# The second block of an expert's tokens: gathered feature-major from split rows, scaled on ScalarE and VectorE, its slots turned later

## The chip, the core and the metric

The kernel runs on one core of a Trainium2 chip. It is timed in device microseconds, as the median of several runs. Besides, one execution was taken by the hardware profiler; its page and trace tell for each engine what it did and what it waited for. The engines are PE (TensorE, with its weight loads as PEld), DVE (VectorE), ACT (ScalarE), POOL (GpSimd) and SP (SyncE, which here issues the weight transfers).

## What is computed

Three transformer layers run over 256 tokens of width 1024: one layer of a first model (grouped attention, spatial gating, cross attention), then two layers of a second model (stick-breaking attention, retention). Each of the three ends in a mixture of 16 experts, of which a token uses two. Cut to what matters here, for the second model:

```python
h = x * (1.0 + scale) + shift                    # per feature
combine = ...                                    # 256 x 16, two nonzero weights a token
for e in range(16):
    hidden = silu(t @ w_gate[e]) * (t @ w_up[e]) # 1024 -> 512
    out = out + combine[:, e:e+1] * (hidden @ w_down[e])   # 512 -> 1024
```

Per expert that is 6 MB of float32 weights, 16 x 3 panels of 2 MB in each expert stage.

## The kernel before

**Stages.** Each of the three expert stages is `moe(L)` with L = 0, 1, 2. It routes the tokens, then walks over eight pairs of experts: `pair(q, k)` with q = 0 to 3 and k = 0, 1. The pairs of q = 0 and q = 3 are written out, those of q = 1 and 2 are a loop. The order of the work is that of the code on each engine, tied together by semaphores; nothing is planned at run time but the routing.

**Slots.** An expert takes its tokens in blocks of at most 64 (`CAP`). The first block of every expert is gathered together with three others: `SELQ` holds for four experts the 0/1 selection of tokens to slots, and `gather_quad` multiplies it with the token rows. For that the normalised rows are held twice in float32r, as a high and a low part (`XHR`, `XLR`), with the features of a chunk side by side. The result comes out with features on partitions, is scaled and shifted from PSUM by ACT and DVE (`quad_out`, L1511 and L2166), and is the stationary operand of the gate and up products (`gate_up`, L871).

**The second block.** An expert with more than 64 tokens gets further blocks. After each pair every engine runs `more` for both experts of the pair (PE L994, ACT L1575, DVE L2244). It reads the number of further blocks from `TBL`, jumps over the block's code if there is none, and else loops over the blocks. DVE has made the block's selection `SELX` beforehand for every expert, needed or not (`choose_more`, L2147). A block goes like this:

1. PE: `gather_more` (L848) multiplies `SELX` with the unsplit float32 rows, which gives 64 slots on partitions by 1024 features, folded into one PSUM bank `B_XG` (4 products, which the trace shows as 8 passes).
2. PE: `turn_more_slots` (L863) turns the selection and collects the slots' weights in bank `B_TR`, for the scatter at the end.
3. ACT: copies the gathered rows to `XROWS` (L1583); later it copies the turned slots out (`swt_more_out`, L1523).
4. PE: `turn_more` (L856) transposes `XROWS` back to features on partitions, four transposes.
5. DVE: `xe_out` (L2179) scales and shifts eight chunks of 128 x 64 into `XEX` (L2186).
6. PE: `gate_up` on `XEX`, into bank `B_GU`: 16 products, in the trace 32 passes of 512 columns.
7. ACT silu (L1588), DVE multiplication (L2251), PE `turn_more_h`, ACT copy (L1590), PE `down_more`, DVE weighting (L2257), ACT and DVE split (L1594, L2263), PE `scatter_more`.

**Weights.** Six ring slots of 2 MB, `ring_lo` and `ring_hi` with three each, hold gate, up and down panels of the two experts of a pair. SP issues a panel's load (L1211) once the old panel in its slot has been read: gate and up after the block's gate and up products, where there is a block, down after its down product. SP waits in a fixed order: gate and up of the first expert, gate and up of the second, then both down panels.

**Records.** Nearly all products have line L419, the helper that issues them; they are told apart by their operands. `Z` in the names stands for one large scratch tensor that holds `SELX`, `XEX` and the hidden rows among others.

Of the kernel before, what the change touches and what calls it, by code (L numbers as in the profile page):

```python
# [20 lines left out]
F32 = mybir.dt.float32  # L21
# [7 lines left out]
P = 128  # L29
# [71 lines left out]
def build(nc, A, out, stop, final_ready):  # L101
# [40 lines left out]
    ZR, ZT = 8960, 11264  # L142
    with nc.sbuf_tensor("Z", [P, 12288], F32) as Z:
        pass
    with nc.sbuf_tensor("Z_before_SELQ", [P, 2560], F32):
        with nc.sbuf_tensor("SELQ", [P, NT, 4 * CAP], F32R) as SELQ:
            with nc.sbuf_tensor("TURN", [P, NT, TURN_COLS], F32R) as TURNER:
                pass
# [183 lines left out]
    def zv(at, *shape):  # L332
        v = Z[:, at:at + int(np.prod(shape))]
        if len(shape) == 2:
            return v.rearrange("p (a b) -> p a b", b=shape[1])
        return v
# [27 lines left out]

    RT = Z[:, 11264:12288]

    SELX = [zv(2048 + 256 * k, NT, P) for k in range(2)]
    free = [3072 + NT * TURN_COLS]

    def cols(n):  # L370
# [27 lines left out]
    def m(L, name):  # L398
        return S(f"m{L}_{name}")
# [17 lines left out]
    def _(pe):  # L417
        def mm(o, l, r, start, stop):
            return nc.tensor.matmul(o, l, r, start=start, stop=stop, skip_group_check=True)  # L419
# [339 lines left out]
        def moe(L):  # L759
# [87 lines left out]

            def gather_more(k):  # L848

                by4 = src[:, :, :].rearrange("p t (i h j) -> p t h i j", h=2, j=4)  # L850
                for t in range(NT):
                    mm(ps[0:CAP, B_XG, :], SELX[k][:, t, 0:CAP], by4[:, t, 0], t == 0, t == NT - 1)
                    ins = mm(ps[CAP:P, B_XG, :], SELX[k][:, t, CAP:P], by4[:, t, 1], t == 0, t == NT - 1)
                ins.then_inc(m(L, "x_xr"), 1)

            def turn_more():  # L856

                by4 = XROWS[:, :].rearrange("p (i j) -> p j i", j=4)
                for j in range(4):
                    ins = nc.tensor.transpose(ps[:, B_XG, j * P:(j + 1) * P], by4[:, j, :], ident)  # L860
                ins.then_inc(m(L, "x_xg"), 1)

            def turn_more_slots(k, done):  # L863
                sel = SELX[k]
                for t in range(NT):
                    ins = nc.tensor.transpose(ps[:, B_TR, t * P:(t + 1) * P], sel[:, t, :], ident)
                for t in range(NT):
                    ins = mm(ps[:, B_TR, SEQ:SEQ + 1], sel[:, t, :], WTOKX[k][:, t:t + 1], t == 0, t == NT - 1)
                ins.then_inc(done, 1)
# [124 lines left out]
            def more(p, k, a, wg, wu, wd, final):  # L994

                e = 2 * p + a
                nb = pe.value_load(TBL[0:1, L, 0, bass.ds(e, 1)], min_val=0, max_val=3)
                b1 = pe.value_load(TBL[0:1, L, 1, bass.ds(e, 1)], min_val=1, max_val=48)
                with pe.If(nb > 0):
                    with pe.Fori(0, nb) as j:  # L1000
                        if k == 0:
                            wait_moe(pe, L, "swt", p + 2)
                            wait_moe(pe, L, "ws", p + 2)
                        elif not final:
                            wait_moe(pe, L, "xe_a", p + 2)
                            wait_moe(pe, L, "xe_v", p + 2)
                        pe.wait_ge(m(L, "x_sel"), b1 + 2 * p + 1 + j)
                        gather_more(a)
                        turn_more_slots(a, m(L, "x_swp"))
                        pe.wait_ge(m(L, "x_xs"), b1 + j)  # L1010
                        turn_more()
                        pe.wait_ge(m(L, "x_xe"), b1 + j)
                        wait_moe(pe, L, "ye", 2 * p + 2)
                        gate_up(B_GU, lambda c: XEX[:, c, :], wg, wu, m(L, "x_gu"), False)
                        pe.wait_ge(m(L, "x_h"), b1 + j)
                        turn_more_h()
                        pe.wait_ge(m(L, "x_ht"), b1 + j)
                        down_more(wd, m(L, "x_y"))
                        pe.wait_ge(m(L, "x_swt"), b1 + j)
                        pe.wait_ge(m(L, "x_ye"), b1 + j)  # L1020
                        scatter_more().then_inc(m(L, "xdone"), 1)
# [265 lines left out]
    def _(act):  # L1287
# [196 lines left out]
        def moe(L):  # L1484
# [90 lines left out]
            def more(p, a):  # L1575

                e = 2 * p + a
                nb = act.value_load(TBL[0:1, L, 0, bass.ds(e, 1)], min_val=0, max_val=3)
                b1 = act.value_load(TBL[0:1, L, 1, bass.ds(e, 1)], min_val=1, max_val=48)
                with act.If(nb > 0):  # L1580
                    with act.Fori(0, nb) as j:
                        act.wait_ge(m(L, "x_xr"), b1 + j)
                        nc.scalar.activation(XROWS[:, :], ps[:, B_XG, :], Copy).then_inc(m(L, "x_xs"), 1)  # L1583
                        act.wait_ge(m(L, "x_swp"), b1 + j)
                        act.wait_ge(m(L, "xdone"), b1 + j)
                        swt_more_out(m(L, "x_swt"))
                        act.wait_ge(m(L, "x_gu"), b1 + j + 1)
                        nc.scalar.activation(SGX[CAP:P, :], ps[0:CAP, B_GU, :], ACT.Silu).then_inc(m(L, "x_sg"), 1)  # L1588
                        act.wait_ge(m(L, "x_htp"), b1 + j)
                        nc.scalar.activation(HTX.rearrange("p c s -> p (c s)"), ps[:, B_GU, 0:SEQ], Copy).then_inc(m(L, "x_ht"), 1)  # L1590
                        act.wait_ge(m(L, "x_yf" if L else "x_y"), b1 + j)
                        act.wait_ge(m(L, "x_swt"), b1 + j)
                        if L:
                            nc.scalar.activation(YH[2], SGX, Copy).then_inc(m(L, "x_yh"), 1)  # L1594
                        else:
                            nc.scalar.activation(YH[2], ps[:, B_Y, :], Copy, scale=WSLOT[2]).then_inc(m(L, "x_yh"), 1)
# [130 lines left out]
    def _(dve):  # L1727
# [336 lines left out]
        def moe(L):  # L2064
# [112 lines left out]
                ins.then_inc(S("moe_ws"), 1)  # L2177

            def xe_out(done):  # L2179
                xg = ps[:, B_XG, :].rearrange("p (j h s) -> p j h s", j=4, h=2)  # L2180
                for c in range(KC):
                    o = xg[:, c % 4, c // 4, :]
                    if shift is None:
                        ins = V.tensor_scalar(XEX[:, c, :], o, gain[:, c:c + 1], None, ALU.mult)
                    else:
                        ins = V.tensor_scalar(XEX[:, c, :], o, gain[:, c:c + 1], shift[:, c:c + 1], ALU.mult, ALU.add)  # L2186
                ins.then_inc(done, 1)
# [56 lines left out]
            def more(e, a, nb, b1):  # L2244

                with dve.If(nb > 0):
                    with dve.Fori(0, nb) as j:
                        dve.wait_ge(m(L, "x_xg"), b1 + j)
                        xe_out(m(L, "x_xe"))
                        dve.wait_ge(m(L, "x_sg"), b1 + j)  # L2250
                        V.tensor_tensor(HH[CAP:P, :], ps[CAP:P, B_GU, :], SGX[CAP:P, :], ALU.mult).then_inc(m(L, "x_h"), 1)  # L2251
                        if L:
# [340 lines left out]
```

## Time and profile before

| | us |
|---|---|
| median of 3 runs | 1489.62 |
| lowest and highest run | 1488.06, 1492.7 |
| span of the profiled execution | 1480.9 |
| PE busy in it | 1320.8 |
| DVE busy | 581.3 |
| ACT busy | 431.7 |

The page gives the profiled execution by its span, from the first to the last instruction; what lies around it is the rest of the device time. A row of the timeline is: start, duration, engine, line, operation, what is written and read, the count, and in brackets the idle time of the engine before it and what ended that. A row of the chain of waits is: start, length, and what the end of the program was waiting for in that time. In the trace the code of a second block is run twice, from 730.5 and from 1412 us; these are called A and B. Busy shares of stages with different limits don't add up to a reason, so rows are read stage by stage.

### The profile page before, as it was taken

What the parts mean: (1) busy time and instruction counts of PE and PEld (TensorE: products, weight loads), DVE (VectorE), ACT (ScalarE), POOL (GpSimd) and SP (SyncE); (2) the same over time, 40 slices, a digit from 0 to 9 for tenths busy, and PEclk for the clock granted to TensorE, in tenths of its full rate; (3) what the DMA queues carried; (4) which work ended last, traced back from release to release, by engine and by line L of the source; (5) the groups of instructions that cost most, each with busy time, mean ns of one, the idle gap of its engine ahead of it and who ended that gap; (6) DMA issues with size and microseconds to landing.
All of it is one profiled execution on the core that took longest, in us unless ns stands there. A gap on an engine that the chain in (4) does not pass through costs nothing.

```text
span 1480.9 us, 20887 instructions
## 1 busy us (share of the span) xinstructions
PE 1320.8 (89%) x7694; PEld 815.7 (55%) x7695; DVE 581.3 (39%) x1234; ACT 431.7 (29%) x693; POOL 410.2 (28%) x190
## 2 busy tenths in 40 slices
PE   7999987889899889998789799789997979889975
PEld 6886775534334389766234334279886853333422
DVE  5598543612112162447214222279007062322224
ACT  4554433211111146443111111145435331111110
POOL 5892643100000067151000000069964710000000
PEclk9999999999999999999899999999999999999998
DMA  7664566999999975518589999976544479999953
GB/s 285 215 201 173 186 228 231 393 402 426 426 428 428 391 283 183 190 58 338 231 344 420 426 422 428 397 269 235 191 150 191 170 321 412 422 416 420 427 221 126
DMA packets 89628, 448.04 MB, mean 303 GB/s; under 512 B 7804, under 2 KB 9768, under 8 KB 70952
## 3 DMA queue, kind: packets, MB, share of 16 engines
q1 hardware_dynamic: 85856, 445.87, 75.4%
q8 instruction: 79, 1.29, 0.4%
q10 hardware_dynamic: 3656, 0.57, 0.3%
q14 instruction: 37, 0.30, 0.1%
HBM read 445.38 MB, written 1.05 MB: 301 GB/s over the span
## 4 chain that ended last, share of the span: by engine, by line
PE 65%; DMA 15%; DVE 9%; issue 4%; POOL 3%; ACT 3%; ACTq 0%; SPq 0%; DVEq 0%; POOLq 0%
PE ps L419 63%; DMA ring_hi<-in_moe_w_up 10%; DMA ring_hi<-in_w_up 3%; POOL WLO L2528 3%; DMA ring_hi<-in_ada_w 1%; ACT WHI L1326 1%; DVE Z L1944 1%; DVE Z L1932 1%; DVE Z L1945 1%; DVE Z L1943 1%; DMA ring_lo<-in_w_ckv 1%; PE ps L884 1%; DMA ring_lo<-in_ret_w_in 1%; DMA ring_lo<-in_w_out 1%; POOL RS L2497 1%
## 5 line engine op out<-in xcount | busy, mean ns | idle before, releaser
L2528 POOL TENSOR_TENSOR WLO<-ring_lo,WHI 128x1024 fp32r<-128x1024 f32 (+1 forms) x154 | 379.3, 2485 | 702.6 <-ACT WHI L1326 700.7
L419 PE MATMUL ps<-ring_hi,Z 128*64 128x512 f32 x1248 | 375.4, 616 | 25.3 <-DMA ring_hi<-in_moe_w_up 14.4
L419 PE MATMUL ps<-ring_lo,Z 128*64 128x512 f32 x1152 | 350.6, 613 | 33.6 <-issue 24.3
L419 PEld LDWEIGHTS ps<-ring_lo,Z 128*64 128x64 f32 x1152 | 111.0, 141 | 248.2 <-issue 234.1
L1326 ACT ACTIVATE WHI<-ring_lo 128x1024 fp32r<-128x1024 f32 (+1 forms) x160 | 165.5, 1048 | 214.1 <-PE ps L419 177.3
L419 PEld LDWEIGHTS ps<-ring_hi,Z 128*64 128x64 f32 x1248 | 119.6, 142 | 153.7 <-issue 147.5
L2195 DVE TENSOR_TENSOR Z<-ps,Z 64x512 f32<-64x512 f32 x48 | 33.1, 689 | 357.4 <-ACT Z L1533 354.2
L1533 ACT ACTIVATE Z<-ps 64x512 f32<-64x512 f32 x48 | 28.4, 591 | 370.4 <-PE ps L419 357.6
L419 PE MATMUL ps<-WHI,HTH 128*128 128x512 f32 x320 | 126.8, 396 | 7.2 <-POOL WLO L2528 3.2
L419 PE MATMUL ps<-WLO,HTH 128*128 128x512 f32 x320 | 125.1, 391 | 0.0
L419 PE MATMUL ps<-WHI,HTL 128*128 128x512 f32 x320 | 125.1, 391 | 0.0
L2497 POOL TENSOR_TENSOR RS<-MS,NEGH 128x1 f32<-128x1 f32 (+2 forms) x26 | 22.2, 856 | 357.8 <-DVE MS L1781 298.7
L419 PE MATMUL ps<-HTH,WHI 128*128 128x256 f32 x320 | 92.2, 288 | 6.6 <-POOL WLO L2528 4.0
L419 PE MATMUL ps<-HTL,WHI 128*128 128x256 f32 x320 | 91.2, 285 | 0.0
L419 PE MATMUL ps<-HTH,WLO 128*128 128x256 f32 x320 | 91.1, 285 | 0.0
L419 PEld LDWEIGHTS ps<-WHI,HTH 128*128 128x128 f32 x320 | 60.5, 189 | 22.5 <-issue 6.3
L419 PEld LDWEIGHTS ps<-WHI,HTL 128*128 128x128 f32 x320 | 60.4, 189 | 12.9
L419 PEld LDWEIGHTS ps<-WLO,HTH 128*128 128x128 f32 x320 | 60.5, 189 | 11.9
L419 PEld LDWEIGHTS ps<-HTH,WHI 128*128 128x128 f32 x320 | 62.1, 194 | 8.4 <-issue 5.0
L419 PEld LDWEIGHTS ps<-HTL,WHI 128*128 128x128 f32 x320 | 62.1, 194 | 0.0
L419 PEld LDWEIGHTS ps<-HTH,WLO 128*128 128x128 f32 x320 | 62.1, 194 | 0.0
L419 PE MATMUL ps<-SELQ,XSPLIT 128*128 128x256 f32 x288 | 50.7, 311 | 5.7 <-DVE SELQ L2144 5.7
(299 smaller groups left out, 1719.2 us busy)
## 6 DMA issues: line engine op xcount, KB each, us to landing
ring_lo<-in_ada_w SPq DMA_DIRECT2D x22, 2048.0 KB, 8.1
ring_lo<-in_moe_w_gate SPq DMA_DIRECT2D x16, 2048.0 KB, 12.1
ring_lo<-in_moe_w_up SPq DMA_DIRECT2D x16, 2048.0 KB, 16.5
ring_lo<-in_moe_w_down SPq DMA_DIRECT2D x16, 2048.0 KB, 12.6
ring_hi<-in_moe_w_gate SPq DMA_DIRECT2D x16, 2048.0 KB, 13.6
ring_hi<-in_moe_w_up SPq DMA_DIRECT2D x16, 2048.0 KB, 18.5
ring_hi<-in_moe_w_down SPq DMA_DIRECT2D x16, 2048.0 KB, 16.9
ring_lo<-in_ret_w_in SPq DMA_DIRECT2D x12, 2048.0 KB, 8.1
```

Of the source, the lines that this page charges most:

```text
L419: return nc.tensor.matmul(o, l, r, start=start, stop=stop, skip_group_check=True)
L884: ins = nc.tensor.transpose(ps[:, bank, c * P:(c + 1) * P], by4[:, c, :], ident)
L1326: nc.scalar.activation(WHI[:, q, 0:size], slot(r)[:, q * size:(q + 1) * size], Copy).then_inc(S("hi_split"), 1)
L1533: nc.scalar.activation(SG[r, :], ps[CAP - CAP * a:P - CAP * a, bank, :], ACT.Silu).then_inc(S("moe_sg"), 1)
L1932: ins = V.tensor_tensor(qk4[:, t, h], qk4[:, t, h], gain, ALU.mult)
L1943: V.tensor_tensor(t1, x0, c1, ALU.mult)
L1944: link(V.tensor_tensor(t2, x1, c2, ALU.mult))
L1945: link(V.tensor_tensor(o, t1, t2, op))
L2195: V.tensor_tensor(HH[r, :], ps[r, bank, :], SG[r, :], ALU.mult).then_inc(S("moe_h"), 1)
L2497: nc.gpsimd.tensor_tensor(RS[:, par, at:at + width], MS[:, par, at:at + width], NEGH[:, 0:width], ALU.pow).then_inc(S("rstd"), 1)
L2528: nc.gpsimd.tensor_tensor(WLO[:, q, 0:size], slot(r)[:, q * size:(q + 1) * size], WHI[:, q, 0:size].bitcast(F32), ALU.subtract).then_inc(S ...
```

## The change

`SELX` becomes a float32r tensor of its own name at the same addresses. The gather of a second block uses it as the moving operand against the split rows: for each of eight feature chunks, two token tiles and the high and low part, one product of 128 x 128 by 64 columns, so 32 in all, which leaves features on partitions at once. Chunks 0 to 3 go to bank `B_XG`, 4 to 7 to `B_TR`, each half with a semaphore of its own. ACT scales the first half into `XEX`, DVE the second. `XROWS`, its copy and `turn_more` are no longer used. The gate and up products wait for ACT's half ahead of chunk 0 and for DVE's half ahead of chunk 4. `turn_more_slots` comes after them, and on ACT silu comes ahead of the copies of the turned slots.

```diff
--- before.py
+++ after.py
@@ -142,6 +142,9 @@
     ZR, ZT = 8960, 11264
     with nc.sbuf_tensor("Z", [P, 12288], F32) as Z:
         pass
+    with nc.sbuf_tensor("Z_before_SELX", [P, 2048], F32):
+        with nc.sbuf_tensor("SELX", [P, 2, NT, P], F32R) as SELX_:
+            pass
     with nc.sbuf_tensor("Z_before_SELQ", [P, 2560], F32):
         with nc.sbuf_tensor("SELQ", [P, NT, 4 * CAP], F32R) as SELQ:
             with nc.sbuf_tensor("TURN", [P, NT, TURN_COLS], F32R) as TURNER:
@@ -364,7 +367,7 @@
 
     RT = Z[:, 11264:12288]
 
-    SELX = [zv(2048 + 256 * k, NT, P) for k in range(2)]
+    SELX = [SELX_[:, k, :, :] for k in range(2)]
     free = [3072 + NT * TURN_COLS]
 
     def cols(n):
@@ -847,21 +850,16 @@
 
             def gather_more(k):
 
-                by4 = src[:, :, :].rearrange("p t (i h j) -> p t h i j", h=2, j=4)
-                for t in range(NT):
-                    mm(ps[0:CAP, B_XG, :], SELX[k][:, t, 0:CAP], by4[:, t, 0], t == 0, t == NT - 1)
-                    ins = mm(ps[CAP:P, B_XG, :], SELX[k][:, t, CAP:P], by4[:, t, 1], t == 0, t == NT - 1)
-                ins.then_inc(m(L, "x_xr"), 1)
-
-            def turn_more():
-
-                by4 = XROWS[:, :].rearrange("p (i j) -> p j i", j=4)
-                for j in range(4):
-                    ins = nc.tensor.transpose(ps[:, B_XG, j * P:(j + 1) * P], by4[:, j, :], ident)
-                ins.then_inc(m(L, "x_xg"), 1)
+                for c in range(KC):
+                    o = ps[:, (B_XG, B_TR)[c // 4], CAP * (c % 4):CAP * (c % 4) + CAP]
+                    for t in range(NT):
+                        for x in (XHR, XLR):
+                            ins = mm(o, x[t][:, P * c:P * c + P], SELX[k][:, t, 0:CAP], c % 4 == 0 and t == 0 and x is XHR, t == NT - 1 and x is XLR)
+                    if c % 4 == 3:
+                        ins.then_inc(m(L, ("x_xga", "x_xgv")[c // 4]), 1)
 
             def turn_more_slots(k, done):
-                sel = SELX[k]
+                sel = SELX[k].bitcast(F32)
                 for t in range(NT):
                     ins = nc.tensor.transpose(ps[:, B_TR, t * P:(t + 1) * P], sel[:, t, :], ident)
                 for t in range(NT):
@@ -1006,12 +1004,15 @@
                             wait_moe(pe, L, "xe_v", p + 2)
                         pe.wait_ge(m(L, "x_sel"), b1 + 2 * p + 1 + j)
                         gather_more(a)
+
+                        def more_in(c):
+
+                            if c % 4 == 0:
+                                pe.wait_ge(m(L, ("x_xea", "x_xev")[c // 4]), b1 + j)
+
+                        wait_moe(pe, L, "ye", 2 * p + 2)
+                        gate_up(B_GU, lambda c: XEX[:, c, :], wg, wu, m(L, "x_gu"), False, more_in)
                         turn_more_slots(a, m(L, "x_swp"))
-                        pe.wait_ge(m(L, "x_xs"), b1 + j)
-                        turn_more()
-                        pe.wait_ge(m(L, "x_xe"), b1 + j)
-                        wait_moe(pe, L, "ye", 2 * p + 2)
-                        gate_up(B_GU, lambda c: XEX[:, c, :], wg, wu, m(L, "x_gu"), False)
                         pe.wait_ge(m(L, "x_h"), b1 + j)
                         turn_more_h()
                         pe.wait_ge(m(L, "x_ht"), b1 + j)
@@ -1579,13 +1580,19 @@
                 b1 = act.value_load(TBL[0:1, L, 1, bass.ds(e, 1)], min_val=1, max_val=48)
                 with act.If(nb > 0):
                     with act.Fori(0, nb) as j:
-                        act.wait_ge(m(L, "x_xr"), b1 + j)
-                        nc.scalar.activation(XROWS[:, :], ps[:, B_XG, :], Copy).then_inc(m(L, "x_xs"), 1)
+                        act.wait_ge(m(L, "x_xga"), b1 + j)
+                        for c in range(4):
+                            o = ps[:, B_XG, CAP * c:CAP * c + CAP]
+                            if shift is None:
+                                ins = nc.scalar.activation(XEX[:, c, :], o, Copy, scale=gain[:, c:c + 1])
+                            else:
+                                ins = nc.scalar.activation(XEX[:, c, :], o, ACT.Identity, scale=gain[:, c:c + 1], bias=shift[:, c:c + 1])
+                        ins.then_inc(m(L, "x_xea"), 1)
+                        act.wait_ge(m(L, "x_gu"), b1 + j + 1)
+                        nc.scalar.activation(SGX[CAP:P, :], ps[0:CAP, B_GU, :], ACT.Silu).then_inc(m(L, "x_sg"), 1)
                         act.wait_ge(m(L, "x_swp"), b1 + j)
                         act.wait_ge(m(L, "xdone"), b1 + j)
                         swt_more_out(m(L, "x_swt"))
-                        act.wait_ge(m(L, "x_gu"), b1 + j + 1)
-                        nc.scalar.activation(SGX[CAP:P, :], ps[0:CAP, B_GU, :], ACT.Silu).then_inc(m(L, "x_sg"), 1)
                         act.wait_ge(m(L, "x_htp"), b1 + j)
                         nc.scalar.activation(HTX.rearrange("p c s -> p (c s)"), ps[:, B_GU, 0:SEQ], Copy).then_inc(m(L, "x_ht"), 1)
                         act.wait_ge(m(L, "x_yf" if L else "x_y"), b1 + j)
@@ -2177,9 +2184,8 @@
                 ins.then_inc(S("moe_ws"), 1)
 
             def xe_out(done):
-                xg = ps[:, B_XG, :].rearrange("p (j h s) -> p j h s", j=4, h=2)
-                for c in range(KC):
-                    o = xg[:, c % 4, c // 4, :]
+                for c in range(4, KC):
+                    o = ps[:, B_TR, CAP * (c % 4):CAP * (c % 4) + CAP]
                     if shift is None:
                         ins = V.tensor_scalar(XEX[:, c, :], o, gain[:, c:c + 1], None, ALU.mult)
                     else:
@@ -2245,8 +2251,8 @@
 
                 with dve.If(nb > 0):
                     with dve.Fori(0, nb) as j:
-                        dve.wait_ge(m(L, "x_xg"), b1 + j)
-                        xe_out(m(L, "x_xe"))
+                        dve.wait_ge(m(L, "x_xgv"), b1 + j)
+                        xe_out(m(L, "x_xev"))
                         dve.wait_ge(m(L, "x_sg"), b1 + j)
                         V.tensor_tensor(HH[CAP:P, :], ps[CAP:P, B_GU, :], SGX[CAP:P, :], ALU.mult).then_inc(m(L, "x_h"), 1)
                         if L:
```

## Rows read from the trace of the kernel before

**Rows 1.** From the page's head: the span and the number of instructions.

```profile
span 1480.9 us, 20887 instructions
```

**Rows 2.** Timeline around block A: start, duration, engine, line, operation, idle time before.

```profile
727.33 0.75 DVE L2203 SCALAR_TENSOR_TENSOR Z<-ps,Z,GB 128x512 f32<-128x512 f32 x1 [1.08 <-PE ps L419]
...
730.54 1.89 PE L419 MATMUL ps<-Z 128*64 128x512 f32 x8
...
732.64 0.50 PE L419 MATMUL ps<-Z 128*128 128x1 f32 x4
...
734.09 0.60 ACT L1583 ACTIVATE XROWS<-ps 128x512 f32<-128x512 f32 x1 [1.91 <-issue]
...
734.84 0.18 ACT L1525 ACTIVATE Z<-ps 128x1 f32<-128x1 f32 x1
...
746.37 0.33 SPq L1211 DMA_DIRECT2D ring_hi<-in_moe_w_gate  x1
...
747.55 0.68 PE L419 MATMUL ps<-CST,Z 64*128 64x64 f32 x2 [1.42 <-DVE Z L2251]
...
748.60 0.38 ACT L1590 ACTIVATE Z<-ps 128x256 f32<-128x256 f32 x1 [1.83 <-PE ps L892]
```

**Rows 3.** Chain of waits through block B: start, length, what.

```profile
1415.50 0.61 ACT XROWS L1583
...
1416.15 1.14 PE ps L860 x4
...
1419.48 8.90 PE ps L419 x32
```

**Rows 4.** Stretches: us, busy PE, PEld, DVE, ACT, POOL, granted clock, DMA share, GB/s.

```profile
720.00:748.00 28.00, 21.24 (x96) 8.11 (x93) 8.95 (x27) 4.62 (x10) 0.00 (x0) 0.94 0.16 59
...
748.00:948.00 200.00, 180.00 (x848) 75.75 (x848) 50.33 (x122) 28.52 (x52) 0.00 (x0) 0.97 1.00 424
...
1412.00:1430.00 18.00, 12.80 (x53) 4.70 (x50) 4.24 (x11) 2.15 (x5) 0.00 (x0) 0.81 0.08 19
```

**Rows 5.** Timeline: block B's gather, and the last pair's second products behind it.

```profile
1411.97 1.89 PE L419 MATMUL ps<-Z 128*64 128x512 f32 x8
...
1446.06 7.04 PE L419 MATMUL ps<-ring_hi,Z 128*64 128x512 f32 x32
```

**Rows 6.** Chain of waits through block A.

```profile
734.74 0.76 PE ps L860 x4
...
735.53 2.12 DVE Z L2186 x8
...
737.69 8.47 PE ps L419 x32
```

**Rows 7.** Timeline: gathers for four experts at once, and ACT's chunk scalings.

```profile
770.79 0.42 PEld L419 LDWEIGHTS ps<-SELQ,XSPLIT 128*128 128x128 f32 x3 [0.81 <-issue]
...
771.26 0.43 PEld L419 LDWEIGHTS ps<-SELQ,XSPLIT 128*128 128x128 f32 x3
...
691.30 4.37 PE L419 MATMUL ps<-SELQ,XSPLIT 128*128 128x256 f32 x24 [1.48 <-DVE SELQ L2144]
...
696.42 1.93 ACT L1511 ACTIVATE Z<-ps,ADA 128x256 f32<-128x256 f32 x4 [6.39 <-PE ps L419]
```

**Rows 8.** A stretch of 1 us, as block A's gate and up products begin.

```profile
737.00:738.00 1.00, 0.31 (x2) 0.29 (x4) 0.63 (x3) 0.00 (x0) 0.00 (x0) 0.52 0.00 0
```

**Rows 9.** PE's timeline: gate and up products after shorter and longer idle time.

```profile
1394.96 7.09 PE L419 MATMUL ps<-ring_hi,Z 128*64 128x512 f32 x32 [1.67 <-DMA ring_hi<-in_moe_w_up]
...
819.03 8.73 PE L419 MATMUL ps<-ring_hi,Z 128*64 128x512 f32 x32 [2.71 <-DMA ring_hi<-in_moe_w_up]
```

**Rows 10.** PE's timeline around jumps over unused block code.

```profile
846.53 8.63 PE L419 MATMUL ps<-ring_lo,Z 128*64 128x512 f32 x32 [5.06 <-issue]
...
1464.83 0.47 PE L419 MATMUL ps<-YHS,SELTS 128*128 128x512 f32 x1 [0.70 <-issue]
...
958.30 0.50 PE L419 MATMUL ps<-YHS,SELTS 128*128 128x512 f32 x1
```

## The prediction

> **What bounds the kernel now.** I read the page's head first, then the timeline and the chain of waits around the changed code, then the busy times in stretches, and last the spacing of the operations that the change adds. The page gives a span of 1480.9 us [rows 1]; the median of the runs is 1489.62, so 8.7 us lie around the span, and I carry them over unchanged. What counts is where the changed code runs. The copy into XROWS (L1583) stands only twice in the trace, at 734.09 and 1415.50 us [rows 2, 3]: of 48 expert visits only two have a second block, one in each expert stage of the second half of the model. Call them A and B. In both the expert is the second of its pair, with its gate and up panels in `ring_hi`.
>
> Is the path through A and B exposed? By two views, yes. In 720 to 748 us the DMA share is 0.16 and in 1412 to 1430 it is 0.08, while in 748 to 948 it is 1.00 at 424 GB/s [rows 4]: the weight stream has run dry because the ring's slots wait for the block. The next gate panel is issued at 746.37 [rows 2], as the block's gate and up products end. So from A on the stream is a queue that starts when A frees its slots, and 200 us of full stream start earlier by whatever A gains. After B the last pair's second pair of products starts at 1446.06 with no idle time before it [rows 5], so no transfer is late there and B's gain goes to the end. The chain of waits runs through both blocks without slack: after the copy four transposes (0.76 us in A, 1.14 in B), in A eight scalings on DVE (2.12), then 8.47 and 8.90 us of gate and up products [rows 3, 6].
>
> **The change, part by part.** *Gather and turn.* Removed are the four float32 gather products (eight recorded passes, 1.89 us from 730.54 [rows 2]), the copy, the four transposes, and half of DVE's scalings. Added are 32 products, each with a load of 128 columns and 64 moving columns. No row has this shape. The nearest are the gathers with the same stationary rows and 256 moving columns: the loads of one chunk's four start at 770.79 and of the next at 771.26, 0.47 / 4 = 0.119 us each; the first gather of that layer took 4.37 for 24, 0.182 each [rows 7]. I take 0.119, because the loads are equal and the moving side is shorter. Less than that I don't count, since the gather's end will not be what ends last. So 32 x 0.119 = 3.8 us: in A from 730.54 to 734.35, in B from 1411.97 [rows 5] to 1415.8; A's first half is there at about 732.6.
>
> ACT can't start on it earlier than it starts on XROWS now: it sat idle 1.91 us for "issue" before 734.09, while the old gather's last pass had ended at 732.43 (730.54 + 1.89) [rows 2]. Its own entry into the block ends last there, not the gather. Four scalings of 128x64 now stand where the copy stood. The chunk scalings of 128x256 take 1.93 for four [rows 7], with the last of about 0.56 so 0.457 apart. The width costs (0.60 - 0.18) / 511 = 0.82 ns a column, from ACT's copies of 512 and of 1 column [rows 2]; 192 columns fewer are 0.16 less. So 0.30 apart and 0.40 for the last: 3 x 0.30 + 0.40 = 1.30 us (bounds 4 x 0.18 = 0.72 and 1.93). With 0.05 until PE wakes the products start at 734.09 + 1.35 = 735.44 instead of 737.69 [rows 6]: **2.25 us in A**; at 1416.85 instead of 1419.48 [rows 3], **2.63 in B**, where the transposes were slower. DVE's four scalings take 2.12 / 2 = 1.06 from the gather's end, till about 735.6; PE wants them after four of eight chunks, 3.5 us into the products, at 739.0. They are covered by 3.4 us, and by over 1 us if the gather takes 0.182 each.
>
> *Clock.* The products of A took 8.47 us because they began at the lower level: granted 0.52 in 737 to 738, that is near 1.2 GHz [rows 8]; those of B took 8.90. After short idle time the same 32 passes take 7.09, as after 1.67 us at 1394.96; after 2.71 us, at 819.03, they take 8.73 [rows 9]. The new idle time is 735.44 - 734.35 = 1.1 us in A and 1.0 in B, which by those rows keeps the clock. Against it: what precedes is narrow work, not full products, and in B the transposes at 1416.15 were already slow (1.14 us), after only 1.58 us of idle time and some narrow products [rows 3]. So I take one of each: A at the upper level (8.47 - 7.12 = **1.35**), B at the price that A pays today (8.90 - 8.47 = **0.43**). Bounds for both together: 0, and 1.35 + 1.78 = 3.13.
>
> *Slots turned later.* Two transposes and four small products follow the old gather, till 733.14 (732.64 + 0.50) [rows 2], 0.8 us, hidden today under ACT's entry. They move behind the products, where PE idles 1.42 us before 747.55, for silu and the multiplication. ACT's two copies of them (the last is that of 1 column, at 734.84) move behind silu and ahead of the copy at 748.60, which had 1.83 us idle before it [rows 2]. Behind PE's turned slots only the transposes queue that wait for the hidden rows, and behind ACT's new wait only that copy. I cost this at nothing; without the cover at 0.8 us a block, 1.6 in all.
>
> *Elsewhere.* SELX in its new type is written by the same DVE instructions in every pair; DVE waits 1.08 us for PE before its next step, at 727.33 [rows 2], so some hundred ns more would be hidden. No DMA is added or moved in its queue; SP's issues follow the same releases.
>
> Sum: 2.25 + 1.35 + 2.63 + 0.43 = **6.66 us**: span 1474.2, time 1489.62 - 6.66 = 1483.0.
>
> **The rivals.** *Clock otherwise.* Low in both as today: 4.88 us, 1484.7. Full in both: 4.88 + 3.13 = 8.0, 1481.6. Both are faster by more than 0.3% (4.5 us), about what a measurement of this kernel can tell from no change.
>
> *The gather ends last.* At 0.182 each it takes 5.8 us: it ends at 736.4 in A and 1417.8 in B, and the gain is 1.3 + 1.7 = 3.0: 1486.6, within 0.3%. For: these products are more load than work, and no row has them. Against: at 0.119 there is 1.1 us to spare.
>
> *Hidden anyway.* If the weight stream decided, nothing would move: 1489.6. The shares of 0.16 and 0.08 speak against it.
>
> *Longer code to skip: slower.* Each visit without a second block jumps over the block's code on PE. Counted by the loads and passes of A in the timeline, this code grows from 158 to 198. Around such jumps PE sometimes stands still for "issue": it is idle 5.06 us before 846.53 [rows 10], where the stream is full and hides it. Exposed are five places: before A and B (the jump over the first expert's block) and the ends of the three expert stages, where the idle time at 1464.83 is 0.70 us today [rows 10]. A stop of 5.06 there is 4.36 more, some 3.7 after what the next wait hides; ahead of a block it starts the gather 5 us late, so the products at 739.4 instead of 735.44. At about 3.9 each, three of the five cost 11.7, less 6.66 is +5.0: **1494.7**. From three on it decides; one or two end between -2.8 and +1.1. For: the row of 5.06. Against: at the end of the middle stage, at 958.30, the jump leaves no idle time today [rows 10], and a quarter more code is little.
>
> The Trainium skill, "Runtime: NRT & Kernel Launch", section Instruction fetch mechanics, states a rule that speaks against this change: a taken branch whose target is outside the pages already fetched waits for a DMA of its page. The same section gives TensorE room for 2048 instructions, and by that a jump over some 200 would seldom pay. The 5.06 us agree with the rule in kind; no row shows which jumps pay.
>
> That the change doesn't do what it says would need other blocks than the two of L1583; routing is decided before this code, and I give that nothing of its own.
>
> **How the numbers follow.** Clock kept in one block 0.34 (forecast, 1483.0), in both 0.20, in none 0.20; gather last 0.10; one or two exposed stops 0.07; hidden 0.03; three or more stops 0.06. Faster by over 0.3%: the first three, 0.74, less 0.02 since 4.88 lies near the bound: 0.72. Within: 0.21. Slower: 0.06, and 0.01 for a bad sample. The range reaches from 1480.3 (clock kept in both, less 1.3 us; the fastest run of before lies 1.6 under the median) to 1487.0 (gather last, and 0.4). The stops and the hidden case, 0.16, and a little of the ends are left out.
>
> **What would show it.** Right: 32 narrow gather passes in about 3.8 us; ACT's first scaling some 3.55 us after the first of them; the products 1.35 us after that, and 7.1 us long where the clock held; the turned slots inside the idle time after the products; transfers issued right behind. Wrong: PE still gathering when ACT is done; products of 8.5 us or more in both blocks; new idle time for "issue" ahead of A, B or a stage's end.

## The result: the blocks got shorter, the program slower

| | before | after |
|---|---|---|
| median us (10 runs each) | 1488.07 | 1492.37 |
| lowest, highest | 1482.02, 1492.7 | 1488.71, 1497.47 |
| profiled execution: time, span | span 1480.9 [rows 1] | 1491.91, 1490.0 |

The ratio is 1.0037 with a 95% interval of 1.0019 to 1.0054: 5.5 us slower (4.3 by the medians), where 1483.0 was forecast. The page of after gives the span, and in its list of DMA queues (packets, MB, share) the queue that fetches instructions; the page of before has 79 packets and 1.29 MB there.

```profile
span 1490.0 us, 20963 instructions
...
q8 instruction: 84, 1.38, 0.4%
```

Block A in the timeline of after (start, length, engine, line, operation, idle time before):

```profile
727.66 0.52 PE L422 MATMUL ps<-SELX,XSPLIT 128*128 128x64 f32 x3
...
731.14 0.28 PE L422 MATMUL ps<-SELX,XSPLIT_last 128*128 128x64 f32 x1
...
731.40 1.29 ACT L1589 ACTIVATE Z<-ps,ADA 128x64 f32<-128x64 f32 x4 [2.21 <-issue]
731.46 1.10 DVE L2192 TENSOR_SCALAR Z<-ps,ADA 128x64 f32<-128x64 f32 x4 [1.48 <-PE ps L422]
...
732.75 8.78 PE L422 MATMUL ps<-ring_hi,Z 128*64 128x512 f32 x32 [1.33 <-ACT Z L1589]
741.46 0.44 PE L864 MATMUL ps<-CST,SELX 128*128 128x128 f32 x2
...
742.95 0.68 PE L422 MATMUL ps<-CST,Z 64*128 64x64 f32 x2 [0.71 <-DVE Z L2257]
```

The answer to [rows 2, 6]. The gather takes 731.14 + 0.28 - 727.66 = 3.76 us, ACT's four scalings 1.29, and the products start 732.75 - 727.66 = 5.09 us after the gather where they started 737.69 - 730.54 = 7.15 after it: the path is 2.06 us shorter. Block B, the answer to [rows 3, 5], and the next expert's first 32 passes behind each block:

```profile
1424.30 1.29 ACT L1589 ACTIVATE Z<-ps,ADA 128x64 f32<-128x64 f32 x4 [1.91 <-issue]
...
1425.64 8.78 PE L422 MATMUL ps<-ring_hi,Z 128*64 128x512 f32 x32 [1.02 <-ACT Z L1589]
...
753.19 9.20 PE L422 MATMUL ps<-ring_lo,Z 128*64 128x512 f32 x32
...
1446.09 9.21 PE L422 MATMUL ps<-ring_lo,Z 128*64 128x512 f32 x32
```

B's gather begins at 1420.86, so its products come 4.78 us later, against 1419.48 - 1411.97 = 7.51 in the kernel before. The products take 8.78 in both blocks, and the 32 passes behind each block take 9.2, where before they took 7.09: the clock is low there (granted 0.78 from 753 to 763, against 1.00 from 756 to 764 before).

So where do 9.1 us of span go? Some 4 to 5 of them belong to the executions that were profiled: 1.9 us lie around the span of after (1491.91 - 1490.0), and with as much the execution of before took about 1482.8, 5 us under its median, where that of after lies 0.5 under its own. Moments of both timelines, each a start on PE:

| from, to | before | after | difference |
|---|---|---|---|
| first instruction, A's gather | 730.54 | 727.66 | -2.9 |
| A's gather, A's scatter | 25.25 | 23.53 | -1.7 |
| A's scatter, last turn of hidden rows of the stage | 192.97 | 197.44 | +4.5 |
| that, the next stage's first transposes | 18.98 | 21.67 | +2.7 |
| those, the last stage's first down products | 265.25 | 265.47 | +0.2 |
| that, B's gather | 178.98 | 185.09 | +6.1 |
| B's gather, B's scatter | 26.05 | 23.23 | -2.8 |
| B's scatter, the last turn | 16.50 | 19.50 | +3.0 |

Both blocks gain, 4.5 us together. The 2.9 us ahead of A lie in stages where no block runs; nothing of the change explains them, and the runs of before spread over 10.7 us. The loss is in the stretches in which *no* block runs: 4.5 + 2.7 + 6.1, and 3.0 after B. The 3.0 are the first passes behind B, later and at the low clock. Behind A PE is as late, but how much of that is in the 4.5 isn't shown, since weights are waited for later in that stretch. In these stretches PE stands still for "issue", and 32 passes right behind a stop can take 9.58 to 10.04 instead of 7.09; four of the rows:

```profile
812.94 10.04 PE L422 MATMUL ps<-ring_lo,Z 128*64 128x512 f32 x32 [3.75 <-issue]
848.01 9.58 PE L422 MATMUL ps<-ring_lo,Z 128*64 128x512 f32 x32 [4.44 <-issue]
961.63 0.47 PE L422 MATMUL ps<-YHS,SELTS 128*128 128x512 f32 x1 [3.39 <-issue]
1246.78 9.87 PE L422 MATMUL ps<-ring_lo,Z 128*64 128x512 f32 x32 [3.92 <-issue]
```

All four lie, by the code's order, right behind jumps over the unused code of further blocks. Counted from 250 us on and at 0.6 us or more each, after has 12 such stops, 36.4 us in all, before 9 of 24.4. The stop at 961.63 is new, where [rows 10] had none (958.30). The lengths of the stops don't add up to the loss: in the first expert stage, from its first gate products to its last down products, they are 13.3 us in after and 8.0 in before, and both take 227.8; in the last stage, up to B, they are 10.4 and 9.2, and the loss there is 6.1. The same stretches by busy time (columns as in [rows 4]), after first, then before:

```profile
751.00:948.00 197.00, 181.32 (x828) 76.28 (x828) 48.43 (x121) 27.51 (x50) 0.00 (x0) 0.94 0.99 411
1235.00:1420.00 185.00, 169.54 (x787) 69.99 (x788) 50.57 (x127) 27.83 (x51) 0.00 (x0) 0.95 0.98 409
```

```profile
755.00:948.00 193.00, 175.78 (x828) 74.27 (x828) 48.78 (x120) 27.50 (x50) 0.00 (x0) 0.97 1.00 424
1233.00:1411.00 178.00, 165.65 (x784) 69.06 (x786) 50.53 (x127) 27.16 (x50) 0.00 (x0) 0.97 1.00 422
```

The work is the same (828 passes); the weight stream falls from 424 to 411 GB/s and the clock from 0.97 to 0.94. The stream isn't independent of PE: in the waits of SP's queue, PE is waited for 142.5 us in 1236 to 1420 of after, 134.5 in 1233 to 1411 of before. So a stop of PE can delay the loads; how much each one did, these rows don't say:

```profile
SPq L1212 <- PE ps L422: 142.5, 17, 12.6
```

### The profile page after: what moved, and what is told of

The parts are those of the page before. It is cut to its first block, busy times and chain, and to the rows that moved or that the text cites. A ratio compares the mean times of both kernels' runs of the same rounds, so it can differ in the third digit from the quotient of the medians.

```text
span 1490.0 us, 20963 instructions
## 1 busy us (share of the span) xinstructions
PE 1332.3 (89%) x7734; PEld 825.3 (55%) x7735; DVE 579.7 (39%) x1226; ACT 433.5 (29%) x699; POOL 410.1 (28%) x190
## 3 DMA queue, kind: packets, MB, share of 16 engines
q8 instruction: 84, 1.38, 0.4%
## 4 chain that ended last, share of the span: by engine, by line
PE 70%; DMA 10%; DVE 9%; issue 4%; POOL 3%; ACT 3%; ACTq 0%; SPq 0%; DVEq 0%; POOLq 0%
PE ps L422 68%; DMA ring_hi<-in_moe_w_up 4%; DMA ring_hi<-in_w_up 3%; POOL WLO L2534 3%; DMA ring_hi<-in_ada_w 1%; PE ps L882 1%; DVE Z L1951 1%; ACT WHI L1327 1%; DVE Z L1939 1%; DVE Z L1952 1%; DVE Z L1950 1%; DMA ring_lo<-in_w_ckv 1%; POOL RS L2503 1%; DMA ring_lo<-in_ret_w_in 1%; DMA ring_lo<-in_w_out 1%
## 5 line engine op out<-in xcount | busy, mean ns | idle before, releaser
L422 PE MATMUL ps<-ring_lo,Z 128*64 128x512 f32 x1152 | 361.6, 631 | 45.9 <-issue 34.9
## 6 DMA issues: line engine op xcount, KB each, us to landing
ring_lo<-in_moe_w_gate SPq DMA_DIRECT2D x16, 2048.0 KB, 11.4
```

## The experiments

Two theories. **Length:** the change makes a copy of the block's PE code 198 recorded loads and passes long instead of 158, each expert stage has 12 copies of it, and 46 of the 48 expert visits jump over one; the longer jumps cost more than the blocks gain. **Executed work:** what the new block does (narrow gather, scaling on two engines, order of the slots, the clock behind it) costs the time. Ratios are to the kernel before, with 95% intervals; "stops" as counted above.

| kernel | records jumped over | blocks that run | ratio | stops, us | instruction packets |
|---|---|---|---|---|---|
| before | 158 | old | 1 | 9, 24.4 | 79 |
| after | 198 | new | 1.0037 (1.0019 to 1.0054) | 12, 36.4 | 84 |
| b_pad40 | 198 | old | 1.0077 (1.0058 to 1.0097) | 12, 40.4 | 85 |
| b_pad120 | 278 | old | 1.0614 (1.0587 to 1.0642) | 20, 115.5 (one, of 0.87, not behind a jump) | 105 |
| b_once120 | 278 in one copy a stage, else 158 | old | 1.0015 (0.9999 to 1.0032) | 10, 30.4 | 80 |
| a_high | 166 | new, half the gather | 0.9964 (0.9950 to 0.9978) | 12, 33.8 | 80 |
| a_158 | 158 | new | 0.9981 (0.9967 to 0.9996) | 8, 19.5 | 79 |
| b_cut | 2 | old | 0.9962 (0.9945 to 0.9978) | 3, 2.8 | 57 |
| a_cut | 2 | new | 0.9930 (0.9906 to 0.9955) | 3, 3.0 | 57 |
| a_merge | 396, for a pair | new | 1.0130 (1.0106 to 1.0154) | 14, 55.5 | 84 |

What a stop waits for is in the traces. Of the 69 stops of 2 us or more, in these kernels and the three further down, 68 have a packet of the instruction queue (q8) starting inside them, and the stop ends behind it; the 69th, in b_once120, has one just ahead of it. Of the 205 idle stretches of PE of that length that something else ended, 23 have one. The 43 shorter stops have one in 2 cases.

### Longer code in the kernel before: b_pad40, b_pad120, b_once120

b_once120 puts the 60 transposes in under one more condition, for the first expert of a stage alone.

```diff
                         pe.wait_ge(m(L, "x_ye"), b1 + j)
+                        with pe.If(nb > 2):        # never so
+                            for i in range(20):    # b_pad120, b_once120: 60
+                                nc.tensor.transpose(ps[:, B_XG, P * (i % 4):P * (i % 4) + P], SELX[a][:, i % NT, :], ident)
                         scatter_more().then_inc(m(L, "xdone"), 1)
```

> The kernel before, with 20 transposes more in the code of every second block on PE (40 loads and passes, as many as the change adds), under a condition that never holds, so that nothing of it is executed. Length of the skipped code: the changed kernel won 4.3 us at its two blocks and came out 4 to 5.5 us slower, so the longer jumps cost 8 to 10 us; this one has the longer jumps without the gain, so 7 to 10 us slower than before. Executed work (clock, order of the new steps): no change, within 2 us. Position of the code on its pages: some us either way, not in proportion to the padding.

> The same with 60 transposes (120 loads and passes) never executed in every second block's code. Length of the skipped code: clearly more than with 40, 15 to 30 us slower. Executed work: no change. Position on the pages: some us either way.

> The kernel before with 60 transposes never executed in one place a layer only, the block code of the first expert, so that all later code of PE is shifted but only one jump a layer is longer. Length of the skipped code: within 2 us of before. Executed work: no change. Position of the code on its pages: a difference of 4 us or more, in either direction.

Code that never runs makes the old kernel 0.77% slower (11.4 us) at the length of the new one, more than the change itself. Sixty transposes cost 91 us, three times the upper end of what was expected: the cost isn't proportional to the length. b_pad40 lies over its 7 to 10 us too. Two stops of b_pad120 in the first expert stage:

```profile
431.99 9.79 PE L419 MATMUL ps<-ring_lo,Z 128*64 128x512 f32 x32 [16.97 <-issue]
...
502.58 7.78 PE L419 MATMUL ps<-ring_lo,Z 128*64 128x512 f32 x28 [9.63 <-issue]
```

The first holds four instruction packets, of 16 KB each (1.38 MB / 84), the second two, so a long stop is several fetches.

b_once120 moves all later code by as much as b_pad120 does in its first copy, and costs nothing that can be told from the interval: by this shift, where code lies is worth at most 0.32%, 4.8 us. It isn't without effect: other jumps stop than before, with 30.4 us instead of 24.4. Other shifts weren't run.

### Shorter code in the changed kernel: a_high, a_158

a_high leaves out the low part of the rows in the blocks' gather, so 16 products instead of 32:

```diff
-                        for x in (XHR, XLR):
-                            ins = mm(o, x[t][:, P * c:P * c + P], SELX[k][:, t, 0:CAP], c % 4 == 0 and t == 0 and x is XHR, t == NT - 1 and x is XLR)
+                        x = XHR
+                        ins = mm(o, x[t][:, P * c:P * c + P], SELX[k][:, t, 0:CAP], c % 4 == 0 and t == 0, t == NT - 1)
```

> The changed kernel with the low part of the split rows left out of the second block's gather: 16 products instead of 32, so the block's code on PE counts 166 loads and passes, near the 158 of before. Length of the skipped code: the gain at the two blocks remains (4.3 us, at most 0.5 more since ACT's entry into the block ends last), so 3 to 6 us faster than before. Executed work: as slow as the changed kernel, 3 to 6 us slower than before. Position on the pages: anything between.

It is 5.3 us faster than before, and faster than both kernels. Its profile, of its fastest execution (1475.93), has nearly as many stops as after all the same, 12 of 33.8 us; but the middle stage from A's scatter to the last turn takes 191.75 us with 10.25 of stops, where after takes 197.44 with 9.34. So the sum of the stops doesn't tell the time; which of them reach it stays open. a_high runs less work too, so a_158 keeps the two blocks that run whole and shortens the other copies alone:

```diff
-                        gather_more(a)
+                        gather_more(a, range(KC) if (L, str(p), a) in ((1, "0", 1), (2, "6", 1)) else (3, 5, 7))
```

> The changed kernel whole where a further block runs (expert 1 of the second expert stage, expert 13 of the third); in the 34 other copies, whose code is only jumped over, 20 of the gather's 32 products are left out, which brings a copy from 198 recorded loads and passes to the 158 of the kernel before. Theory 'length of skipped code': the two blocks keep the 4.3 us that they gained by the two traces, and the jumps cost what they cost before: 3 to 6 us faster than before (ratio 0.996 to 0.998). Rival 'work that is executed' (the gather's products, their scaling, the clock after them): nothing that runs is different from the changed kernel, so it stays 4 to 7 us slower than before (1.003 to 1.005).

0.9981, 2.8 us faster than before (0.6 to 4.9): what runs is the changed kernel, instruction for instruction, and only code that is never run is gone. Against the changed kernel that is 1.0037 - 0.9981 = 0.56%, 8.3 us. The executed-work theory falls here: it asked for 1.003 to 1.005. Nor was it a better clock: in this trace the blocks took 24.10 and 23.93 from gather to scatter, in after 23.53 and 23.22, and the 32 passes behind them 9.09 and 9.15, in after 9.20 and 9.21. The gain is a little smaller than the expected 0.996 to 0.998.

### Nearly nothing to jump over: b_cut, a_cut

```diff
             def more(...):
                 ...
+                if (L, str(p), a) not in ((1, "0", 1), (2, "6", 1)):
+                    with pe.If(nb > 0):
+                        nc.tensor.transpose(ps[:, B_XG, 0:P], SELX[a][:, 0, :], ident)
+                    return
                 with pe.If(nb > 0):
```

> The kernel before, whole where a further block runs; in the 34 other copies one transpose stands in place of the block's code, with its count's read and its jump kept. Theory 'length of skipped code': the nine stops of TensorE's own sequencer after 250 us, 24.4 us in all, go away nearly all, and with them the time that the weights' transfers lose behind them: 8 to 25 us faster than before (0.983 to 0.995). Rival: the stops are hidden by the weights' transfers, and only code beyond some length costs: within 3 us of before (0.998 to 1.002).

> The changed kernel with the same cut in the 34 copies that are only jumped over. Theory 'length of skipped code': as b_cut, less the 4.3 us that the two blocks gain, so 3 to 6 us below b_cut. Rival 'work that is executed': 4 to 7 us above b_cut.

b_cut gains less than the 0.983 to 0.995 expected: 24.4 us of stops cost 5.6 us, so most of their length was hidden. Nearly all stops are gone in both, and of 79 and 84 instruction packets 57 are left. In the timeline of a_cut, the places of the stops at 848.01 and 961.63 of after; ahead of the second PE now waits for DVE instead:

```profile
836.66 7.09 PE L422 MATMUL ps<-ring_lo,Z 128*64 128x512 f32 x32 [1.09 <-issue]
...
953.59 0.50 PE L422 MATMUL ps<-YHS,SELTS 128*128 128x512 f32 x1 [1.17 <-DVE YLS L2219]
```

This gives the two prices apart. The jumps cost the old kernel 1 - 0.9962 = 0.38%, 5.6 us, and the changed one 1.0037 - 0.9930 = 1.07%, 15.9 us: **10.3 us more**. The blocks alone, with the jumps out of the way, gain 0.9962 - 0.9930 = 0.32%, **4.8 us** (6.3 by the medians of 1479.58 and 1473.29). 10.3 - 4.8 = 5.5 us is the result again, by construction. The intervals are about 0.2% wide to each side, so each of these sums is good to some 3 to 5 us; the price of the longer jumps by the other runs is 8.3 us (a_158 against after) and 11.4 (b_pad40).

### One jump for two experts: a_merge

```diff
-                for a in range(2):
-                    more(p, k, a, wg[a], wu[a], wd[a], final)
+                ...                                # nb, b1: read here for both experts
+                with pe.If(nb[0] + nb[1] > 0):
+                    for a in range(2):
+                        more(p, k, a, wg[a], wu[a], wd[a], final, nb[a], b1[a])
```

> The changed kernel with one jump for a pair of experts where it had two: both counts are read first, and only where their sum is over zero are the two blocks' jumps come to. Half as many jumps, each over about 396 recorded loads and passes. If a jump out of the code at hand costs a wait of its own, however far it goes: faster than the changed kernel by 4 to 10 us. If the cost grows with the code that is jumped over (60 transposes more in a copy cost about 92 us, 20 more about 12): at 792 for a pair's two copies of after's length nothing is saved, 0 to 30 us slower than the changed kernel.

14 us slower than the changed kernel (1.0130 - 1.0037 = 0.93%). Half as many jumps bring more stops, 14 at 24 jumps (22 over a pair's code, and one over a single block in each of the two pairs that have a block); three in the middle stage:

```profile
790.71 7.09 PE L422 MATMUL ps<-ring_lo,Z 128*64 128x512 f32 x32 [3.56 <-issue]
820.35 10.07 PE L422 MATMUL ps<-ring_lo,Z 128*64 128x512 f32 x32 [5.50 <-issue]
855.90 9.37 PE L422 MATMUL ps<-ring_lo,Z 128*64 128x512 f32 x32 [4.90 <-issue]
```

So a stop isn't a fixed price of any jump. Over 2 records 3 of 46 jumps show one, none over 1.1 us; over 158 it is 9, over 198 12, over 278 19, and over 396 14 of 24. But the lengths of the stops don't follow: up to 5.50 us here, 16.97 in b_pad120. The long ones there hold two and four instruction packets, those of a_merge at most one; why 278 leads to several stays open.

### The parts of the change: a_cut_fill, a_cut_dve, a_cut_slots

All three start from a_cut, where the stops don't disturb. a_cut_fill gives PE work in the two idle stretches of a block:

```diff
+                        for i in range(3):
+                            mm(ps[0:CAP, B_GU, :], SELX[a].bitcast(F32)[:, 0, 0:CAP], wg[:, i, :], True, True)
                         gate_up(B_GU, lambda c: XEX[:, c, :], wg, wu, m(L, "x_gu"), False, more_in)
...
                         down_more(wd, m(L, "x_y"))
+                        for i in range(6):
+                            mm(ps[0:CAP, B_GU, :], HTX[:, i % 4, :], wd[:, i % 4, 0:512], True, True)
```

> a_cut (the changed kernel with 34 copies cut to one transpose), and in the two blocks that run TensorE gets work for its idle stretches: three 512-column products between the gather and the gate and up products (it idles 1.3 us there in a_cut's first block, 1.0 in its second) and six between the down products and the scatter (3.1 us idle in each). Theory 'the idle stretch drops the clock': the block's gate and up products take about 7.1 us where a_cut's took 8.78 in both blocks, and the next expert's first 32 passes 7.1 where a_cut's took 8.78 and 9.20; the first is a gain of up to 1.7 us in a block, the second shows in the time only where the weights have landed: 0 to 5 us below a_cut (ratio to before 0.989 to 0.993). Rival 'the clock there follows something else': durations stay between 8.4 and 9.5 us in at least one of the blocks, and the time within 2 us of a_cut.

0.9955 (0.9938 to 0.9973), slower than a_cut and outside what either theory expected: the filling was sized too large. Its passes started 0.85 us apart in A, a time in which the gate and up products behind them do two, so all but the first of A's products came from 736.90 on, 3.85 us after ACT's half was done (731.76 + 1.29). But the trace answers the question. In B the filling goes without a gap to the products, the granted clock is 1.00 throughout, and 31 of the 32 passes take 7.40. In A PE is never idle either, and yet (columns as in [rows 4]):

```profile
728.00:731.50 3.50, 3.50 (x30) 3.48 (x29) 1.44 (x2) 0.63 (x1) 0.00 (x0) 0.90 0.03 7
731.50:737.00 5.50, 5.50 (x14) 2.38 (x14) 1.10 (x4) 1.29 (x4) 0.00 (x0) 0.50 0.00 0
```

The clock falls to 0.50, the lower level of 1.2 GHz, while the narrow gather still runs, and stays there under full-width passes. So idle time isn't all that drops it; the rival holds for A. The next expert's passes take 7.09 behind both blocks, as the theory said; but behind a_cut_slots' blocks, which weren't filled, they do so too, so that proves nothing.

a_cut_dve scales all eight chunks on DVE:

```diff
                         dve.wait_ge(m(L, "x_xga"), b1 + j)
-                        xe_out(m(L, "x_xev"))
+                        xe_out(m(L, "x_xea"), 0)
+                        dve.wait_ge(m(L, "x_xgv"), b1 + j)
+                        xe_out(m(L, "x_xev"), 1)
...                                                # ACT's four scalings go
```

> a_cut with all eight chunks scaled on VectorE and none on ScalarE ('scaled on two engines' undone). By the rows of a_cut four chunks take VectorE 1.10 us and ScalarE 1.29. Theory 'the two halves run side by side and ScalarE ends last': the products wait for the first four on VectorE, which are ready before the gather's second half ends, and then for the last four, some 1.1 to 1.4 us after the gather; since the products begin on chunk 0 they start up to 1.3 us earlier than in a_cut and then wait inside for chunk 4 at most a few tenths: 0 to 1.2 us a block below a_cut, time within 2.5 us of a_cut. Rival 'two engines are needed': products end over 0.5 us later than in a_cut in each block.

0.9925 (0.9904 to 0.9945), the same as a_cut within the intervals. DVE has the first half ready as the gather ends, so the products start without idle time, 0.67 us earlier after the pair's last product in A and 1.10 in B. B's products in a_cut, and A's and B's in a_cut_dve:

```profile
1407.14 8.78 PE L422 MATMUL ps<-ring_hi,Z 128*64 128x512 f32 x32 [1.03 <-ACT Z L1593]
```

```profile
732.32 9.66 PE L422 MATMUL ps<-ring_hi,Z 128*64 128x512 f32 x32
...
1408.07 7.09 PE L422 MATMUL ps<-ring_hi,Z 128*64 128x512 f32 x32
```

B's products keep the upper level without the gap, 7.09; A's lose it all the same. The second engine brings nothing here: in B of a_cut ACT's half is gathered at 1404.33, but ACT begins its scalings at 1405.80, with 1.91 us idle for "issue", and they are the longer ones (1.29 against 1.10).

a_cut_slots turns the slots ahead of the products again:

```diff
+                        pe.wait_ge(m(L, "x_xev"), b1 + j)
+                        turn_more_slots(a, m(L, "x_swp"))
                         gate_up(B_GU, lambda c: XEX[:, c, :], wg, wu, m(L, "x_gu"), False, more_in)
-                        turn_more_slots(a, m(L, "x_swp"))
...                                                # and ACT's copies of the slots ahead of its silu
```

> a_cut with the slots turned ahead of the gate and up products, once VectorE has read the bank, and ScalarE's two copies of them ahead of its silu (the third part of the change undone). The turning takes 0.78 us on TensorE and the two copies 0.97 on ScalarE by the rows of a_cut. Theory 'turning later moves nothing by itself' (the prediction's): the turning falls into the wait for ScalarE's half, the products start within 0.5 us of a_cut and the block's end within 0.5. Rival 'it saves the turning': the products start 0.6 to 0.9 us later and the scatter as much; 1 to 2 us above a_cut in all.

The products start 1.78 us later in A and 0.87 in B, so the rival is right on the path: the turning isn't free ahead of them, since it must wait for DVE to read the bank. The time is 0.9919 (0.9899 to 0.9938), no worse than a_cut. The passes behind the blocks took 7.09 there and 8.78 and 9.20 in a_cut; behind B that gave 3.0 us back in this profile (16.51 from scatter to last turn, against 19.50), behind A next to nothing (190.50 against 190.64).

## Why the prediction was wrong, point by point

- **Two blocks, on the exposed path: right.** They alone were changed in what runs, and with the jumps out of the way they gain 4.8 us of time.
- **Products' start: right in size.** Forecast 2.25 and 2.63. By the span from the gather to the products it is 2.06 and 2.73; ACT's own entry and four scalings set it (1.29 against 1.30 forecast), and the gather isn't last (3.76 against 3.8): a_high's gathers took 1.97, and its products began 5.09 and 4.77 us after their start all the same.
- **Clock: mis-sized.** The sum had 7.12 in A and 8.47 in B, a gain of 1.78. Both took 8.78: 0.31 lost in A against [rows 6], 0.12 gained in B against [rows 3]. What failed here is that the new idle time of 1.1 us keeps the clock: it was read from [rows 9], where full-width products came before. a_cut_fill and a_cut_dve show that in A it falls with no idle time at all. The price behind the block, 9.2 instead of 7.09 in both, wasn't in the sum. It isn't the new block's alone: the passes there took 8.78 behind both old blocks of b_pad40 and 7.09 behind both new ones of a_high. What sets it stays open.
- **Slots turned later: nothing in the time, right;** on the path it is worth 0.87 us in B, as the reordered run shows, not nothing.
- **Gather last, hidden anyway: fell.** The gather ended 1.3 us ahead of the products.
- **Longer code to skip: the step that failed, and this decides.** It stood at nothing in the sum and was given 0.06. The mechanism was put rightly, but three steps of its price were wrong. First, that the stream is full and hides stops within a stage. Much is hidden: before the change 24.4 us of stops cost 5.6. But not all: the middle stage loses 4.5 us by the trace, part of it perhaps to the clock behind A, and the last one 6.1; with the jumped-over code cut they take 190.64 and 177.62 instead of 197.44 and 185.09. Second, that only five places are exposed and three of them must stop: one (961.63) was enough beside the stages' loss. Third, "a quarter more code is little": 10.3 us more. With that term the forecast of the blocks (4.88 with the clock low) ends at 1489.62 - 4.88 + 10.3 = 1495.0, near the rival's 1494.7 and, from the later median of 1488.07, 1493.5 against 1492.37. That comes near the rival's time by luck: of its five exposed places one has a stop, not three.
- **What lies around the span** is some 1.9 us and not 8.7: the profiled execution of before was a fast one. The forecast was a difference from the median, so it doesn't hang on this.

The rule weighed in the prediction stands in the Trainium skill, "Runtime: NRT & Kernel Launch", section Instruction fetch mechanics: a taken branch to a page not yet fetched waits for its transfer. These runs agree: stops and instruction packets fall together, 12 and 84 to 3 and 57, and 68 of 69 longer stops have a packet in them. The same section of the Trainium skill gives TensorE room for 2048 instructions. That room doesn't protect here: jumps over 158 recorded loads and passes already cost 5.6 us, so the measurement decides against the reading that a jump over some 200 would seldom pay.

## What to carry to other kernels

Code that is only jumped over has a price: count how many copies of a conditional block are walked past, and test the change once with those copies cut, before judging what runs. Look for "issue" ahead of PE behind each jump, and don't call such a stop hidden because the DMA share reads 1.00; see whether the queue that issues the transfers waits for the same engine. Don't add the stops up either: 24.4 us of them cost 5.6, and a_high is fast with 33.8. Time the kernel without the jumped-over code. A better path inside a rare block has to pay for its extra instructions at every visit that doesn't need it.

## What was not expected of the hardware

- Jumps over 278 recorded loads and passes cost 91 us more than over 158, over 198 about 11 more (both in the old kernel). Single stops are up to 16.97 us, with four instruction packets in that one; a stop of one packet ends 1.3 to 3.3 us after it, in all but one case. Why the step from 198 to 278 is so large isn't explained.
- Products of 64 columns follow each other every 0.11 us: the loads of one chunk's four start at 728.10, of the next at 728.54. The forecast had 0.119.
- PE's clock fell to the lower level inside such a stream: in a_cut_fill three of its passes together take 0.50 us up to 730.28 and 0.79 from 730.73, while PE was busy 3.50 of 3.50 us. In a_158 and a_merge, which run the same block code, both gathers took 4.46 to 4.50 us instead of 3.76.
- Passes behind a stop of 3.75 us took 10.04 instead of 7.09, so that on PE this stop cost nearly twice its length.
